# Attention of a streaming encoder as one run of 72 units instead of four groups of 18

## What is computed

```python
z = rmsnorm(x) @ w_in                     # aq, ak, av, bq, bk, bv, blr, gate
s = einsum(qb, kb) * 64 ** -0.5 - slopes * dist
p = softmax(concat([s, sink]))[..., :-1]
ao = einsum(p, vb)
y = concat([ao, bo]) * silu(gate)         # bo: the gated linear attention branch
x = x + y @ w_out
```

## Time and profile before

| | us |
|---|---|
| median of three runs | 1598.69 (1594.52 to 1599.26) |
| the profiled execution, its own time | 1598.26 |
| its span in the trace | 1596.2 |
| attention, first scores to first work of the next stage | 137.67 to 476.49 |
| first scores of groups 0, 1, 2, 3 | 137.67, 228.77, 320.98, 409.14 |

### The profile page before, as it was taken

One profiled execution on the slowest core, in us unless ns is written; L12 is line 12 of the kernel. 1 busy time (PEld: TensorE's weight loads), 2 busy tenths in 40 slices (PEclk: granted clock), 3 DMA queues, 4 the chain that ended last, 5 costly groups with the idle time before them and its releaser, 6 DMA issues.

```text
span 1596.2 us, 24860 instructions
## 1 busy us (share of the span) xinstructions
PE 1523.5 (95%) x9622; PEld 1432.1 (90%) x9622; DVE 927.8 (58%) x1423; ACT 456.1 (29%) x808; POOL 689.6 (43%) x466
## 2 busy tenths in 40 slices
PE   6998999999989999999999999989999999989997
PEld 5997777777769999999999999989999999989996
DVE  7114867777775454744459111378887878985113
ACT  5111423333353222122133000225335143362001
POOL 5252212222212333523435444556666565656553
PEclk9999999999999999999999999999999999999998
DMA  4210010100000111110112332111111111113223
GB/s 181 89 60 27 27 42 16 39 26 29 27 29 32 34 32 45 40 34 30 34 44 68 104 101 95 54 55 53 53 40 53 53 40 54 53 53 106 86 81 112
DMA packets 29330, 89.16 MB, mean 56 GB/s; under 512 B 3600, under 2 KB 8784, under 8 KB 29264
## 3 DMA queue, kind: packets, MB, share of 16 engines
q1 hardware_dynamic: 19632, 64.27, 12.1%
q10 hardware_dynamic: 9632, 23.91, 4.6%
HBM read 76.64 MB, written 11.67 MB: 55 GB/s over the span
## 4 chain that ended last, share of the span: by engine, by line
PE 56%; DVE 8%; issue 4%; POOL 2%; ACT 2%; ACTq 0%; POOLq 0%; DVEq 0%
PE ps L388 41%; PE ps L433 6%; POOL w_hi L349 1%; DVE Y L1598 1%; PE ps L707 1%; PE ps L562 1%; POOL w_lo L353 1%; PE ps L628 1%; PE ps L612 1%; PE ps L623 1%; DVE arena L1616 1%; DVE Yr L1383 1%; DVE arena L1613 1%; DVE arena L1621 1%; DVE arena L1619 1%
## 5 line engine op out<-in xcount | busy, mean ns | idle before, releaser
L349 POOL TENSOR_TENSOR w_hi<-raw,ones 128x512 fp32r<-128x512 f32 x226 | 333.1, 1474 | 864.1 <-PE ps L388 484.1
L388 PE MATMUL ps<-H,w_hi 128*128 128x364 f32 x2796 | 568.6, 331 | 23.3 <-DVE H L1171 15.2
L388 PEld LDWEIGHTS ps<-H,w_hi 128*128 128x128 f32 x2796 | 479.5, 189 | 27.0 <-issue 16.4
L388 PE MATMUL ps<-H,w_lo 128*128 128x364 f32 x1716 | 379.6, 330 | 0.0
L353 POOL TENSOR_TENSOR w_lo<-raw,w_hi 128x512 fp32r<-128x512 f32 x226 | 349.5, 1547 | 17.7
L388 PEld LDWEIGHTS ps<-H,w_lo 128*128 128x128 f32 x1716 | 300.2, 189 | 0.0
L562 PE MATMUL ps<-H,w_hi 128*128 128x364 f32 x672 | 148.0, 347 | 0.0
L388 PE MATMUL ps<-Yr,w_hi 128*128 128x364 f32 x636 | 140.7, 329 | 0.0
L907 ACT ACTIVATE arena<-arena,sm 128x256 f32<-128x256 f32 (+1 forms) x144 | 69.6, 484 | 225.3 <-DVE sm L1282 225.3
L433 PE MATMUL ps<-w_hi,H 128*128 128x256 f32 (+1 forms) x720 | 132.4, 284 | 1.6 <-POOL w_lo L353 1.0
L1520 DVE TENSOR_TENSOR arena<-ps,arena 128x1092 f32 (+1 forms) x15 | 19.4, 1295 | 195.3 <-PE ps L388 195.3
(11 more groups left out here) (202 smaller groups left out, 1894.0 us busy)
## 6 DMA issues: line engine op xcount, KB each, us to landing
raw<-weights SPq DMA_DIRECT2D x113, 512.0 KB, 3.3
arena<-xT ACTq DMA_DIRECT2D x15, 546.0 KB, 5.0
x_scratch<-arena ACTq DMA_DIRECT2D x8, 546.0 KB, 5.3
arena<-x_scratch ACTq DMA_DIRECT2D x8, 546.0 KB, 3.6
arena<-k_scratch ACTq DMA_DIRECT2D x8, 304.0 KB, 4.3
yT<-arena SPq DMA_DIRECT2D x2, 768.0 KB, 4.4
yT<-arena SPq DMA_DIRECT2D x2, 576.0 KB, 3.3
k_scratch<-Y ACTq DMA_DIRECT2D x2, 512.0 KB, 2.7
```

What stands on the lines that cost most here:

```text
L349: pool.tensor_tensor(w_hi[:, s, cols].rearrange("p (k n) -> p k n", n=P), raw[:, s, cols].rearrange("p (k n) -> p k n", n=P), every_tile_ones,
L388: mm = pe.matmul(sets[st][:, c, 0:CW], lw[:, s, w], rx[:, k, c * CW:(c + 1) * CW], start=(first and n == 0 and m == 0), stop=(last and n = ...
```

## The change

All four groups become one run of 72 units, written out without a hardware loop. Step S of PE does the scores of unit S, the transposes of S-2 and the values of S-3 with no regard to the border of a group. The blocks of the next group take 5, 4, 5 and 4 steps (`A_STEPS`), 18 together; in the steps of 4 there are 6 tiles each. The keys get a second buffer, filled in step 2 of the group before (it was step 17 of the group before), and so do the values, copied in step 12 of the group before (it was at the border). The copies of sinks and slopes into `cur_sink` go; the instructions read the tables at fixed offsets. The second query block of a group is drained by DVE in step 0 of that group; only scores of b = 1, from step 9 on, read it. Ahead of attention the blocks of group 0 change sets (1, 0, 1, 0 instead of 0, 1, 0, 1), so that its last block, the second query block, lies in set 0, and the first scores wait for the block before it alone; group 0's values are copied between the two gates.

```diff
+ALL_UNITS = A_KV * ATT_UNITS
+A_STEPS = (5, 4, 5, 4)
+A_ENDS = (5, 9, 14, 18)
...
-        kk = part(2184, KW)
-        Vg = part(4616, 10, 64)
+        keys = (part(2184, KW), part(5256, KW))
+        Vgs = (part(4616, 10, 64), part(9096, 10, 64))
...
-                in_block(1 - n % 2, n % 2, PC_A + n, USE_A[n % 2] + n // 2)
-            pe.wait_ge(v_free, NT)
-            pe.wait_ge(drained[1], USE_A1[1])
+                in_block(1 - n % 2, 1 - n % 2, PC_A + n, USE_A[1 - n % 2] + n // 2)
...
-                for s in range(ATT_UNITS + 3):
-                    if s < ATT_UNITS:
-                        scores(s, U + s)
-                    if 0 <= s - 2 < ATT_UNITS:
-                        transposes(s - 2, U + (s - 2))
-                    if s >= 3:
-                        mix_values(s - 3, U + (s - 3))
...
+            def block_step(g, s):
+
+                if g < A_KV - 1:
+                    n = sum(s >= e for e in A_ENDS)
+                    steps, f = A_STEPS[n], s - (A_ENDS[n] - A_STEPS[n])
+                else:
+                    n, steps, f = s // K0_STEPS, K0_STEPS, s % K0_STEPS
+                piece = PC_A + A_PCS * (g + 1) + n
+                if f == 0:
+                    pe.wait_ge(drained[0], USE_A1[0] + 4 * g + n)
+                x0, x1 = (-(-3 * KD * e // steps) for e in (f, f + 1))
...
+            for S in range(ALL_UNITS + 3):
+                g, s = S // ATT_UNITS, S % ATT_UNITS
+                if S == 0:
+                    pe.wait_ge(drained[1], USE_A1[1])
+                if S < ALL_UNITS:
+                    if s == 0:
+                        pe.wait_ge(kk_in, 32 * g + 32)
+                        if g:
+                            pe.wait_ge(drained[0], USE_A1[0] + 4 * g - 1)
+                    if s == NT:
+                        pe.wait_ge(drained[0], USE_A1[0] + 4 * g)
+                    scores(s, S)
...
+                if 0 <= S - 2 < ALL_UNITS:
+                    transposes((S - 2) % ATT_UNITS, S - 2)
+                if S >= 3:
+                    if s == 3:
+                        pe.wait_ge(vg_ready, g + 1)
+                    mix_values((S - 3) % ATT_UNITS, S - 3)
+                if g < A_KV - 1 or g == A_KV - 1 and s < 2 * K0_STEPS:
+                    block_step(g, s)
...
-                    if more and s == ATT_UNITS - 1:
+                if g < A_KV - 1:
+                    if s == 2:
                         load_keys(g + 1)
+                    if s in A_ENDS[0:2]:
+                        gate_tanh_of(0, USE_A1[0] + 4 * g + A_ENDS.index(s) + 1)
...
-                dve.tensor_copy(cur_sink[:, 0, :], vecs[:, bass.ds(VC_SINK + 4 * g, 4)])
-                dve.tensor_copy(cur_sink[:, 2, :], consts[:, bass.ds(CC_SLOPE + 4 * g, 4)])
-                dve.tensor_copy(cur_sink[:, 1, :], nsink[:, bass.ds(4 * g, 4)]).then_inc(sink_cur, 1)
...
+            gate_in(1, PC_A, None)
+            gate(0)
             dve.wait_ge(v_free, NT)
             dve.wait_ge(vcache_in, 16)
...
+            group_values(0)
+            gate_in(0, PC_A + 1, 1)
+            gate(1)
+            for n in range(2):
+                q_in(n, 1 - n, PC_A + 2 + n)
+            for S in range(ALL_UNITS + 4):
+                g, s = S // ATT_UNITS, S % ATT_UNITS
+                if S >= 4:
+                    gate_outputs(S - 4)
...
+                if 0 < g < A_KV and s == 0:
+                    q_in(1, 0, PC_A + A_PCS * g + 3)
+                if g < A_KV - 1:
+                    if s in A_ENDS[0:2]:
+                        n = A_ENDS.index(s)
+                        gate_in(0, PC_A + A_PCS * (g + 1) + n, 2 * g + n + 2)
+                    if s == A_ENDS[2]:
+                        q_in(0, 0, PC_A + A_PCS * (g + 1) + 2)
+                if S < ALL_UNITS:
+                    maxima(S)
+                if 0 <= S - 1 < ALL_UNITS:
+                    normalize(S - 1)
+                if g < A_KV - 1:
+                    if s in (A_ENDS[0] + 1, A_ENDS[1] + 1):
+                        gate(2 * g + 2 + (s > A_ENDS[1]))
+                    if s == 12:
+                        group_values(g + 1)
```

More of the change, by code:

```diff
@@ L572, in _ @@
-            with pe.Fori(0, A_KV - 1) as g:
-                attend(g, A_PCS, 5)
-            attend(A_KV - 1, 2, K0_STEPS)
+            def block_step(g, s):
[8 more added lines that the diff above has]
+                x0, x1 = (-(-3 * KD * e // steps) for e in (f, f + 1))
+                for x in range(x0, x1):
+                    k, m = x // 3, x % 3
+                    if k % 4 == 0 and m == 0:
+                        pe.wait_ge(w_split, 2 * piece + (k // 4 + 1))
+                    lw, rx = ((w_hi, H_hi), (w_lo, H_hi), (w_hi, H_lo))[m]
+                    for c in range(NCH):
+                        mm = pe.matmul(sets[0][:, c, 0:CW], lw[:, 1 - n % 2, k * P:(k + 1) * P],
+                                       rx[:, k, c * CW:(c + 1) * CW], start=(x == 0), stop=(x == 3 * KD - 1))
+                    if (k, m) == (3, 2):
+                        mm.then_inc(half_done, 1)
+                if f == steps - 1:
+                    mm.then_inc(piece_done, 1)
@@ L851, in load_keys @@
                 for j in range(2):
[L852 removed]
+                    act.dma_start(keys[g % 2][A_DIM * j:A_DIM * (j + 1), :], k_all[g]).then_inc(kk_in, 16)
             act.wait_ge(k_all_in, 80)
@@ L896, in _ @@
             act.activation(cur_b[:, 0:1], vecs[:, VC_BLR:VC_BLR + 1], ACT.Copy).then_inc(bias_ready, 1)
[L898 to L914, removed]
-                    if more and s == ATT_UNITS - 1:
-                        load_keys(g + 1)
[L917 to L933, removed]
@@ L1302, in _, with group_values, gate_outputs @@
-            for n in range(2):
-                gate_in(n, PC_A + n, n or None)
-                gate(n)
-            for n in range(2):
-                q_in(n, n, PC_A + 2 + n)
+            def group_values(g):
+                dve.tensor_copy(Vgs[g % 2][:, 0:9, :], V[:, 0:9, A_DIM * g:A_DIM * (g + 1)])
+                dve.tensor_copy(Vgs[g % 2][0:64, 9, :], V[0:64, 9, A_DIM * g:A_DIM * (g + 1)]).then_inc(vg_ready, 1)
+            def gate_outputs(U):
+                g, u = U // ATT_UNITS, U % ATT_UNITS
+                t, b = unit(u)
+                r = tile_rows(t)
+                dve.wait_ge(o_done, U + 3)
+                dve.wait_ge(gated, 2 * g + 2)
+                y = slot(Y, 2 * g + b, t * P, t * P + r)
+                dve.tensor_tensor(y, ps[:, 7, 0:r], y, ALU.mult).then_inc(o_free, 1)
@@ new lines, in normalize @@
+            def normalize(U):
+                t, r3 = unit(U % ATT_UNITS)[0], U % 3
+                r = tile_rows(t)
+                c0, c1 = key_cols(t)
+                dve.wait_ge(exp_done, U + 1)
+                dve.tensor_tensor(sm[0:r, r3, 8:10], sm[0:r, r3, 8:10], sm[0:r, r3, 6:8], ALU.add)\
+                   .then_inc(den_done, 1)
+                dve.wait_ge(den_done, U + 1)
+                dve.reciprocal(sm[0:r, r3, 10:12], sm[0:r, r3, 8:10]).then_inc(rcp_done, 1)
+                dve.wait_ge(rcp_done, U + 1)
+                for j in range(2):
+                    last = dve.tensor_scalar(Ssb[0:r, r3, j, c0:c1], Ssb[0:r, r3, j, c0:c1],
+                                             sm[0:r, r3, 10 + j:11 + j], 0.5, ALU.mult, ALU.mult)
+                last.then_inc(p_done, 1)
```

170 lines of the change are left out of this document (69 added, 101 removed).

## The result

| | kernel before | changed kernel |
|---|---|---|
| median, us | 1598.97 (4 runs) | 1577.92 (4 runs, 1575.24 to 1580.09) |
| ratio | | 0.9873 [0.9855, 0.9892] |
| the profiled execution | 1598.26 | 1579.12 |
| last filling triple ahead of attention to first work of the next stage | 134.14 to 476.49 | 133.33 to 456.62 |

The profiled executions differ by 19.1 us, where 19.2 were forecast; the medians by 21.1. Of the 19.1 the attention stage holds 342.35 - 323.29 = 19.1. Ahead of it the trace of after is 0.8 us quicker, behind it 1.0 slower. The slow stretches of the clock lie at other places there: the trace of before has one at 476 to 482 us, just behind attention, and the trace of after has one at 790 to 798. Over all eleven traces of this case that rest takes 1117.7 to 1123.5 us, and the kernels with and without holes at the borders lie mixed in it.

What follows compares the result with a forecast made beforehand. PE was taken to set attention's pace, the gain being its idle and slow time. Terms 7.2 + 1.8 + 2.2 + 7.2 + 0.8 = 19.2 us off 1598.26 gave 1579 us, range 1571 to 1588.

Steps and rivals of the forecast that it cites:

- The borders: Three borders between attention groups: PE's holes of 2.35, 2.35 and 2.46 us before first scores go, 7.2 us gained.
- Rival D: PE still waits at borders, for the drain instead of the copies: 1581.5 us; inside the forecast's 0.78, no own chance.
- The start: Start of attention: first scores run during DVE's drain, so the block behind them starts 1.8 us earlier.
- The refill: PE's transpose waits behind borders: 1.67 becomes 0.95 us in groups 1 and 2, plus 0.75 in group 3; 2.2 us gained.
- The signs: Trace signs of being right, among them waits of about 0.95 us before transposes in steps 3 and 12 of each group.
- The half clock: PE's half-speed stretches behind the start and borders go, that of group 0's step 3 stays: 7.2 us gained.
- rival C: Clock doesn't follow: half the slow clock stays, 4.2 us lost, 1583 us; inside the forecast's 0.78, no own chance.
- Steps 5 to 8: PE's 0.26 us wait for ACT's copy in step 6 goes through a sixth tile, three times: 0.8 us gained.
- the 0.32 moves to step 10 and stays: PE's 0.32 us wait in step 11 was to move to step 10 and remain, with no gain.
- The added work: Value copies in step 12, key loads in step 2 and longer written-out code cost 0; copies if exposed 4.3 us.
- Rival A: DVE becomes the next wait in attention: 8.9 of the 19.2 us lost, 1588 us; chance 0.13 for 1585 to 1592.
- B: Port lock: each of 28 POOL splits costs PE 1.67 us, 1616 us, slower; chance 0.04 together with code reading.

Runs made afterwards that it cites:

- the kernel with the hole put back: Changed kernel with value copies behind the second query block's drain and first scores of groups 1 to 3 waiting for both: 1592.76 us, 0.9981.
- The kernel with the late signal: Changed kernel with the half-piece signal given three tiles later in five-step blocks, so POOL splits 1.5 us later: 1571.65 us, 0.9847.
- the code written out: Kernel before with its PE, ACT and DVE attention loops written out and nothing else changed: 1598.32 us, 1.0016.
- border wait: Changed kernel with first scores of groups 1 to 3 waiting again for the drained second query block: 1583.65 us, 0.9932.
- copies: Changed kernel with value copies in step 0 behind the drain instead of step 12 of the group before, no added waits: 1580.65 us, 0.9918.
- start: Changed kernel with the old start: group 0's blocks in sets 0, 1, 0, 1, values copied last, first scores waiting for all: 1583.12 us, 0.992.

## Why the prediction was right

**The borders** (7.2 forecast): 7.2. All three holes are gone, and PE waits for no drained query block at them. The one wait of that kind, 0.97 us at the start, is the one that the next term counts on. Rival D is ruled out by the timeline, and the kernel with the hole put back shows that most of the gain was here, together with the clock.

**The start** (1.8): 3.95 - 2.05 = 1.9. The 0.15 us that the term gives to the semaphore were 0.05 (the drain ends at 135.33, the block starts at 135.38).

**The refill** (2.2): groups 1 and 2 wait 0.95 in step 3 instead of 1.67, as worked out from the place of the half; that this comes of the merged steps and not of the missing hole, the trace with the whole hole shows. What the split meets is another thing each time: in step 3 of groups 0 to 2 of the kernel before, and still of group 0, it met two small DVE instructions (1.16 and 1.24 us instead of 0.16, at 329.82 and 331.09 in group 2) and PE waited 1.67; in the merged steps it meets the scalings and PE waits 0.95. Group 3's 0.63 and 0.26 are gone (0.9 for 0.75). Sum 2.3. The kernel with the late signal bears out that the split makes these waits, and shows that 6.4 more could have been had. The signs named the wait in step 3 and 12 of each group; group 3 of the changed kernel has none of 0.95, only 0.38 and 0.23.

**The half clock** (7.2): in this pair of traces the stretches behind the start and the borders went and that of group 0's step 3 stayed, as assumed: 152.39 - 133.92 = 18.5 us to step 4, against 17.0 in the other trace of the same kernel, so the stretch costs 1.5. The assumption was lucky for that one: it fell in one of two executions. What stood before was chance as well: the clock fell behind two of three holes at borders in that trace, and behind one of three in the trace with the code written out. With no fall in the trace of after the term would have been 8.7, so the size of the match is luck; that no slow stretch remains at a border is not, it holds in all seven traces of kernels without the hole. That rules out rival C. And one thing was left out: attention's end. From the last scores (L494 in before, L495 after) to the next stage it took 476.49 - 466.30 = 10.2 us before and 456.62 - 444.75 = 11.9 after, with the granted clock at 0.78 and 0.80 in the two stretches of four us between 446 and 454 us; 1.7 us went back. The second trace of the changed kernel has 10.2, so this too is chance of the execution.

**Steps 5 to 8** (0.8): the 0.26 us are gone three times. The 0.32 three times, which I let stay and moved to step 10, are gone too, 1.0 us not forecast. The step of the prediction that failed is "the 0.32 moves to step 10 and stays".

**The added work** (0): the copies, the keys' loads and the longer code cost nothing that a trace shows.

The sum of what the trace shows: 7.2 + 1.9 + 2.3 + 7.2 + 0.8 + 1.0 - 1.7 = 18.7, of 19.1 measured in the stage; the 0.4 left I can't place. Two misses of opposite sign, 1.0 and 1.7, partly cancel, so that the forecast of 19.2 came closer than its terms. The medians give 21.1 in the first measurement and 19.0 in the last. Rival A had its small part right (every wait left in groups 0 to 3 ends on DVE, up to attention's end) and its price wrong. For B each of the 28 splits had to cost PE 1.67 us; six cost 0.94 to 1.66.

## What to carry to other kernels

A border between groups costs its hole and, in many executions, a stretch at half clock behind it; both go once what the next group needs first has a second buffer and is made early, and a wait that must remain is put behind work of its own engine. To see what the merging itself gives, compare steps of both kinds less tiles and waits: here PE's own work stayed the same, and what the merged steps and the new dealing of tiles gave was shorter waits, 1.3 us in a full group. Then look for two engines that meet at one place of each period: here one signal, given three tiles later, was worth 5 us by the medians.

## What the runs showed of the hardware

*The split and DVE.* POOL's multiplication or subtraction of 128 x 512 (1.3 us) holds up DVE's scalings from SBUF to SBUF and its small instructions with two SBUF inputs, which wait to its end (two scalings took 2.68 us instead of 0.62; two small ones at step 3 of group 0 took 1.14 and 1.23 instead of 0.16), but not its products with an operand in PSUM (0.87) nor its maxima (0.69). That is the lock which the Trainium skill states ("SBUF — State Buffer", section "🔬 SBUF: two separate sides"); by that rule, the trace agrees. In the changed kernel the split starts 0.1 us ahead of the scalings; that starting it 1.5 us later is enough is shown, how little would do is not.

*The clock.* Leaving out attention's end, in nine traces (before, the changed kernel twice, and the runs with the code form, border wait, copies, start, full hole, late signal), behind a PE hole of 2.35 to 3.0 us the clock fell in 9 of 12 cases; behind one of 1.66 to 1.68 us in 6 of 12, and five of these six are among the seven that had a hole of over 2.3 us some 12 to 15 us ahead of them; behind one of 0.94 to 1.43 us, more than 40 times, never. A fall cost 1.4 to 1.6 us in the cases that can be told apart, and 2.6 in one (the first border of the whole hole). At attention's end PE waits 1.58 us and then three times 0.5 to 0.7 within some 8 us, and there the clock fell in 7 of all eleven traces; in two of them (before, late signal) only behind the last of the short ones. So short holes in a row can go with a fall where a single one of 0.95 never did. Why equal holes differ from one execution to the next is left open.
